# Attention heads of two key-value groups in turn, value products of both interleaved, and norm squares moved ahead of the forms

## The chip, the cores and the metric

One core of a Trainium2 chip runs the whole program. The metric is device microseconds of one execution, the median over runs; lower is better. The engines are TensorE (PE; its weight loads are PEld), VectorE (DVE), ScalarE (ACT), GpSimd (POOL) and SyncE (SP), which issues the transfers. Each works through its own list of instructions in order and waits on semaphores that others count up.

## The reference

A two-layer encoder trunk over two sequences, 528 and 272 tokens long (512 and 256 plus 16 learned meta tokens), width 1024, all in fp32. Cut to what matters here:

```python
for layer in range(2):
    h = h + 0.5 * swiglu(rms_norm(h, norm_ffn1[layer]), gate, up, down)   # width 2816
    hn = rms_norm(h, norm_mix[layer])
    h = h + (even_mixer(hn, ...) if layer % 2 == 0 else fourier_mixer(hn, ...))
    h = h + 0.5 * swiglu(rms_norm(h, norm_ffn2[layer]), gate, up, down)
return rms_norm(h, norm_final)[:, N_META:]
...
# even_mixer: attention of 8 heads of 64, heads 0-3 share key-value group 0, heads 4-7 group 1,
# window of 128 to either side, ALiBi bias, and a sink logit of each head in the softmax:
s = einsum(q, k) * scale + bias
m = maximum(max(s), sink); p = exp(s - m); denom = sum(p) + exp(sink - m)
o = einsum(p, v) / denom
```

The attention's result and a pooling mixer are concatenated and go through one output projection.

## The kernel before

Activations lie transposed: channels on the 128 partitions, 800 tokens along the free axis (h has 8 tiles of channels). Large products are three fp32r matmuls of high and low parts (w_hi, w_lo, and the same of the activations). ScalarE makes the high parts, VectorE the low ones.

The four feed-forward networks (f = 0 to 3) compute gate and up products by a Strassen scheme of seven products per tile of 128 columns (22 tiles), from sums of token and channel blocks ("forms" T1, T2, T3, N4, each with a high and a low part). The first two tiles of each network (the lead) are plain products: `plain_unit(j, u)`, 24 matmuls each and four per tile. They cover the making of the forms and of the norm: ScalarE squares the 8 channel tiles (`squares`), VectorE adds them (`add_square`, seven additions), TensorE sums over partitions (`statistics`), VectorE makes the variance, GpSimd raises it to -0.5 (`power`), VectorE spreads it to a diagonal (`diagonal`, into acth), TensorE broadcasts it (`broadcast`), VectorE copies it to rstd (`spread`). For f = 1 and 2 (EARLY) the squares are made in the stage before. For f = 0 and 3 they are made in the lead (`late_squares`), between the other steps of `lead`, in an order written out by hand on ScalarE and VectorE. There TensorE runs the four units of tile 0, the statistics, unit 0 of tile 1, the broadcast, and units 1 to 3; unit 2 waits for rstd. `weights_to(k)` on either engine makes the high or low parts (and sums) of the weights up to a few units ahead of k.

The attention works through 8 tiles of up to 128 queries (ATT_TILES; 256, 384, 384, 272 and 144 keys for the first sequence, 256, 272 and 144 for the second; the tiles of 144 keys have 16 queries), 8 heads each: 64 units u, in quads of four. For each unit: TensorE makes the scores (L1654; q_sb and k_sb hold group 0 in partitions 0 to 63 and group 1 in 64 to 127) into one of three banks; VectorE adds the bias and takes the maximum (L1357), per quad the negated maximum (L1366); ScalarE the exponential with its sum (L865) and that of the sink (L870); VectorE the denominator (L1380), its reciprocal and the scaling (L1387, `norm_quad`); TensorE transposes blocks of 128 keys (L1668) into one of two banks; ScalarE copies them to prob_t (L883, L886); and per quad TensorE multiplies by v (L1689, `times_v`), four heads side by side in up to 512 columns, output in partitions 64 times the group. TensorE's list runs the scores 8 units ahead of the transposes:

```python
for u in range(NU + AHEAD):
    if u < NU:
        scores(u)
    v = u - AHEAD
    if v >= 0:
        transposes(v)
        if v % 4 == 1 and v > 4:
            times_v(v // 4 - 1)
```

ScalarE's list is the exponentials of quad q, then the copies of quad q - 1. VectorE's is three scores of quad q, `norm_quad(q - 1)`, the fourth score, the negated maximum. Score buffer u % 8 is free when transposes(u - 8) are done. Banks 5 to 7 take the value products; from there ScalarE and VectorE write mx_hi and mx_lo (L893, L1394). Behind the attention come the pooling products (L1718 to L1722) and the output projection.

Of the kernel before, what the change touches and what calls it, by code (L numbers as in the profile page):

```python
# [8 lines left out]
P = 128  # L9
# [205 lines left out]
def build(nc, x, gains, sinks, ident_in, alibi_in, edges_in, pool_w_in, tables, gate_up, down5, down6,  # L215
# [18 lines left out]
    def as32(ap):  # L234
# [41 lines left out]
    projected = 6 * T + 4 * POOL_W  # L276
    (_, xn_hi, xn_lo, q_sb, k_sb, v_sb, u_pad, _, mx_hi, mx_lo) = scope([
        ("w_lo_m", [P, WL], f32),
        ("xn_hi", [P, KD, T], f32r), ("xn_lo", [P, KD, T], f32r),
        ("q_sb", [P, 4, T], f32), ("k_sb", [P, T], f32), ("v_sb", [P, T], f32),  # L280
        ("u_pad", [P, 4, POOL_W], f32), ("fill_m", [P, 2 * XF - 2 * KD * T - projected], f32),
        ("mx_hi", [P, KD, T], f32r), ("mx_lo", [P, KD, T], f32r)])
    (_, v_tok, prob_t, score, row_max, neg_max, sink_d, row_sum, sink_e, rden) = scope([
        ("w_lo_a", [P, WL], f32),
        ("v_tok", [P, len(ATT_TILES), P], f32), ("prob_t", [P, 2, 3, 4, P], f32),
        ("score", [P, SCORES, KEYS], f32), ("row_max", [P, 2, 4], f32), ("neg_max", [P, 2, 4], f32),
# [190 lines left out]
    norm_done = sem("norm_done")  # L477
    quad_out = sem("quad_out")
    mix_hi_done = sem("mix_hi_done")
# [29 lines left out]

    UNITS = [(i, hd) for i in range(len(ATT_TILES)) for hd in range(N_HEADS)]  # L510

# [110 lines left out]
    def _(act):  # L622
# [119 lines left out]
        def lead(f):  # L742

            n0, n1, J = GU[f][0], GU[f][1], f * FF_TILES
            early = f in EARLY
            weights_to(n0)
            late_squares(f, 0, 3)
            t1_gain(f)
            weights_to(n0 + 1)
            late_squares(f, 3, 5)  # L750
            form_high(f, "T1")
            late_squares(f, 5, 7)
            weights_to(n0 + 2)
            form_high(f, "T2")
            late_squares(f, 7, KD)
            weights_to(n0 + 3)
# [116 lines left out]
        def prob_copy(u):  # L873
            i = u // 8
            rows = ATT_TILES[i][3]
            k0, k1 = keys_of(i)
            q, c = divmod(u, 4)
            act.wait_ge(prob_t_ps, u + 1)
            if c == 0 and q >= 2:
                act.wait_ge(quad_out, q - 1)  # L880
            full, kr = divmod(k1 - k0, P)
            if kr:
                A.activation(prob_t[0:kr, q % 2, full, c, 0:rows],  # L883
                             banks[0:kr, 3 + u % 2, full * P:full * P + rows], ACT.Copy)\
                    .then_inc(prob_t_done, 1)
            A.activation(prob_t[:, q % 2, 0:full, c, 0:rows],  # L886
                         banks[:, 3 + u % 2, 0:full * P].rearrange("p (j r) -> p j r", r=P)[:, :, 0:rows],
                         ACT.Copy).then_inc(prob_t_done, 1)

        def out_hi(i):  # L890
            s0, L, t, rows = ATT_TILES[i]
            act.wait_ge(quad_out, 2 * i + 2)
            A.activation(mx_hi[:, 0:4, s0 + t:s0 + t + rows],  # L893
                         banks[:, 5 + i % 3, :].rearrange("p (k r) -> p k r", k=4)[:, :, 0:rows],
                         ACT.Copy).then_inc(mix_hi_done, 1)
# [58 lines left out]
    def _(dve):  # L954
# [186 lines left out]
        def ffn(f, norm_before, norm_after):  # L1141
# [40 lines left out]
            def lead():  # L1182

                n0, n1, J = GU[f][0], GU[f][1], f * FF_TILES
                early = f in EARLY
                weights_to(n0)
                late_squares(f, 0, 3)
                t1_sum(f)
                weights_to(n0 + 1)
                late_squares(f, 3, 5)  # L1190
                t2_sum(f)
                if early:
                    variance(norm_before)
                late_squares(f, 5, 7)
                weights_to(n0 + 2)
                if early:
                    diagonal(norm_before)
                form_low(f, "T1")
                late_squares(f, 7, KD)
                weights_to(n0 + 3)  # L1200
                if early:
# [141 lines left out]
        def score_quad(q):  # L1343
# [5 lines left out]
            for c in range(4):  # L1349
                u = 4 * q + c  # L1350
                hd = u % 8
# [5 lines left out]
                V.tensor_tensor_reduce(out=score[0:rows, u % SCORES, 0:k1 - k0],  # L1357
                                       in0=banks[0:rows, u % 3, 0:k1 - k0],
                                       in1=alibi[0:rows, hd, off:off + k1 - k0], scale=1.0,
                                       scalar=sink[0:rows, hd:hd + 1], op0=ALU.add, op1=ALU.max,  # L1360
                                       accum_out=row_max[0:rows, q % 2, c:c + 1])\
# [28 lines left out]
        def tile_lo(i):  # L1390
# [3 lines left out]
            V.tensor_tensor(mx_lo[:, 0:4, s0 + t:s0 + t + rows],  # L1394
                            banks[:, 5 + i % 3, :].rearrange("p (k r) -> p k r", k=4)[:, :, 0:rows],
                            as32(mx_hi[:, 0:4, s0 + t:s0 + t + rows]),
# [86 lines left out]
    def _(pe):  # L1483
# [163 lines left out]
        def scores(u):  # L1647
# [11 lines left out]
        def transposes(u):  # L1659
# [6 lines left out]
            for j in range((k1 - k0 + P - 1) // P):  # L1666
                kr = min(P, k1 - k0 - j * P)
                ins = M.transpose(banks[0:kr, 3 + u % 2, j * P:j * P + rows],  # L1668
                                  score[0:rows, u % SCORES, j * P:j * P + kr],
                                  ident[0:rows, 0:rows])  # L1670
            ins.then_inc(prob_t_ps, 1)

        def times_v(q):

            i = q // 2
            s0, L, t, rows = ATT_TILES[i]
            k0, k1 = keys_of(i)
            side = 64 * (q % 2)
            pe.wait_ge(prob_t_done, TCOUNT[4 * q + 4])
            if q == 0:  # L1680
# [251 lines left out]
```

## Time and profile before

| | |
|---|---|
| median of 3 runs | 2569.61 us (2568.35 to 2571.15) |
| profiled execution | 2569.58 us, span 2567.8 us |
| mean granted TensorE clock | 0.98 |
| busy: PE, DVE, ACT | 98%, 63%, 39% of the span |
| chain that ended last | PE 74%, issue 20%, DVE 3%, ACT 2% |
| attention stage | 641.6 to 757.6 us |
| opening of network 0, of network 3 | first 62 us; about 2010 to 2065 us |

The span is the time from the first to the last instruction of one execution on the chip; the profiled execution's own time is 1.8 us longer. Time on the chain that ended last is what a change can shorten; work of an engine beside it costs nothing. The granted clock is 1.00 at 2.4 GHz and 0.50 at 1.2 GHz.

### The profile page before, as it was taken

What the parts mean: (1) busy time and instruction counts of PE and PEld (TensorE: products, weight loads), DVE (VectorE), ACT (ScalarE), POOL (GpSimd) and SP (SyncE); (2) the same over time, 40 slices, a digit from 0 to 9 for tenths busy, and PEclk for the clock granted to TensorE, in tenths of its full rate; (3) what the DMA queues carried; (4) which work ended last, traced back from release to release, by engine and by line L of the source; (5) the groups of instructions that cost most, each with busy time, mean ns of one, the idle gap of its engine ahead of it and who ended that gap; (6) DMA issues with size and microseconds to landing.
All of it is one profiled execution on the core that took longest, in us unless ns stands there. A gap on an engine that the chain in (4) does not pass through costs nothing.

```text
span 2567.8 us, 35298 instructions
## 1 busy us (share of the span) xinstructions
PE 2504.8 (98%) x13740; PEld 2425.3 (94%) x13740; DVE 1621.7 (63%) x2858; ACT 1001.7 (39%) x1913; POOL 80.9 (3%) x85
## 2 busy tenths in 40 slices
PE   7999999999999999999999999999999899999997
PEld 7999999999449999999999999999999799999996
DVE  7665766753544757575677656665755775666574
ACT  5433433431553434242444433342443443434341
POOL 0000000014000000000000000000002100000000
PEclk9999999999889999999999999999999899999998
DMA  3211121221001121112121112121121211211121
GB/s 119 74 66 58 66 83 52 81 96 53 14 1 50 50 75 60 64 66 72 61 71 62 60 64 74 66 66 66 69 68 47 84 58 66 74 66 66 66 70 64
DMA packets 28532, 166.26 MB, mean 65 GB/s; under 512 B 3408, under 2 KB 3664, under 8 KB 16080
## 3 DMA queue, kind: packets, MB, share of 16 engines
q1 hardware_dynamic: 28368, 164.02, 18.3%
q8 instruction: 110, 1.80, 0.3%
q14 instruction: 54, 0.44, 0.1%
HBM read 160.73 MB, written 3.28 MB: 64 GB/s over the span
## 4 chain that ended last, share of the span: by engine, by line
PE 74%; issue 20%; DVE 3%; ACT 2%; DMA 0%; POOL 0%; POOLq 0%; DVEq 0%; SPq 0%; ACTq 0%
PE banks L1497 28%; PE banks L1576 12%; PE banks L1575 12%; PE banks L1574 12%; PE banks L1593 3%; PE banks L1490 2%; PE banks L1654 2%; PE banks L1689 1%; PE banks L1668 1%; ACT xf_hi L687 1%; DVE xf_lo L1027 0%; DVE sum_sq_x L1013 0%; PE banks L1526 0%; PE banks L1536 0%; DVE w_lo L981 0%
## 5 line engine op out<-in xcount | busy, mean ns | idle before, releaser
L1575 PE MATMUL banks<-xf_lo,w_hi 128*128 128x400 f32 (+2 forms) x2240 | 766.9, 342 | 0.0
L1576 PE MATMUL banks<-xf_hi,w_lo 128*128 128x400 f32 (+2 forms) x2240 | 765.0, 342 | 0.0
L1574 PE MATMUL banks<-xf_hi,w_hi 128*128 128x400 f32 (+2 forms) x2240 | 764.2, 341 | 0.0
L643 ACT ACTIVATE w_hi<-raw 128x512 fp32r<-128x512 f32 (+3 forms) x572 | 314.6, 560 | 365.5 <-PE banks L1497 365.5
L1576 PEld LDWEIGHTS banks<-xf_hi,w_lo 128*128 128x128 f32 x2240 | 422.4, 189 | 0.0
L1575 PEld LDWEIGHTS banks<-xf_lo,w_hi 128*128 128x128 f32 x2240 | 420.5, 188 | 0.0
L1574 PEld LDWEIGHTS banks<-xf_hi,w_hi 128*128 128x128 f32 x2240 | 420.1, 188 | 0.0
L1497 PE MATMUL banks<-act_hi,w_lo 128*128 128x400 f32 (+2 forms) x1408 | 366.4, 341 | 0.0
L1497 PE MATMUL banks<-act_lo,w_hi 128*128 128x400 f32 (+2 forms) x1408 | 366.2, 341 | 0.0
L1497 PE MATMUL banks<-act_hi,w_hi 128*128 128x400 f32 (+2 forms) x1408 | 365.7, 341 | 0.0
L981 DVE TENSOR_TENSOR w_lo<-raw,w_hi 128x512 fp32r<-128x512 f32 (+3 forms) x572 | 343.9, 615 | 19.5 <-ACT w_hi L643 19.4
L643 ACT ACTIVATE w_hi<-w_sum 128x512 fp32r<-128x512 f32 x336 | 209.9, 629 | 304.3 <-DVE w_sum L973 117.8
L1497 PEld LDWEIGHTS banks<-act_hi,w_hi 128*128 128x128 f32 x1408 | 258.5, 188 | 0.0
L1497 PEld LDWEIGHTS banks<-act_lo,w_hi 128*128 128x128 f32 x1408 | 258.1, 188 | 0.0
L1497 PEld LDWEIGHTS banks<-act_hi,w_lo 128*128 128x128 f32 x1408 | 258.0, 188 | 0.0
L981 DVE TENSOR_TENSOR w_lo<-w_sum,w_hi 128x512 fp32r<-128x512 f32 x336 | 229.5, 686 | 2.1 <-ACT w_hi L643 2.1
L1168 DVE TENSOR_TENSOR act_lo<-act,act_hi 128x800 fp32r<-128x800 f32 (+2 forms) x88 | 86.1, 979 | 175.9 <-ACT act_hi L740 175.9
L1137 DVE SCALAR_TENSOR_TENSOR h<-banks,h 128x392 f32<-128x392 f32 (+3 forms) x224 | 72.5, 383 | 133.2 <-PE banks L1497 133.2
L1131 DVE SCALAR_TENSOR_TENSOR h<-banks,h 128x800 f32<-128x800 f32 x64 | 63.4, 990 | 134.1 <-PE banks L1497 134.1
L790 ACT ACTIVATE g<-banks 128x400 f32<-128x400 f32 (+2 forms) x80 | 40.1, 501 | 208.7 <-PE banks L1576 208.7
L965 DVE TENSOR_TENSOR w_sum<-raw 128x512 f32<-128x512 f32 x80 | 55.0, 687 | 81.3 <-PE banks L1497 50.5
L740 ACT ACTIVATE act_hi<-act 128x800 fp32r<-128x800 f32 (+2 forms) x88 | 75.3, 856 | 35.4 <-DVE act L1162 35.4
(179 smaller groups left out, 2711.7 us busy)
## 6 DMA issues: line engine op xcount, KB each, us to landing
raw<-gate_up_dram SPq DMA_DIRECT2D x86, 1024.0 KB, 4.8
raw<-down_dram SPq DMA_DIRECT2D x32, 768.0 KB, 4.2
raw<-down_dram SPq DMA_DIRECT2D x32, 640.0 KB, 3.8
raw<-w_in_dram SPq DMA_DIRECT2D x5, 1024.0 KB, 4.8
raw<-w_fourier_dram SPq DMA_DIRECT2D x8, 576.0 KB, 3.8
raw<-w_out_dram SPq DMA_DIRECT2D x4, 1024.0 KB, 4.8
h<-x_dram SPq DMA_DIRECT2D x8, 400.0 KB, 7.2
y_dram<-h SPq DMA_DIRECT2D x8, 400.0 KB, 2.5
```

What stands on the lines that cost most here:

```text
L643: A.activation(w_hi[:, n % NS, 0:u.cols], source, ACT.Copy).then_inc(w_hi_done, 1)
L740: A.activation(act_hi[:, t, 0:W], act32[:, t, 0:W], ACT.Copy).then_inc(act_hi_done, 1)
L965: ins = V.tensor_tensor(out, quarter(u, "A21"), quarter(u, "A22"), ALU.add)
L981: V.tensor_tensor(w_lo[:, n % NS, 0:u.cols], source, as32(w_hi[:, n % NS, 0:u.cols]), ALU.subtract).then_inc(w_ready, 1)
L1131: return V.scalar_tensor_tensor(two(h[:, m, :]), slot(2 + m % 2), 0.5, two(h[:, m, :]), ALU.mult, ALU.add)
L1137: last = V.scalar_tensor_tensor(h[:, m, t:t + n], banks[:, 4 + 2 * (m % 2) + half, c:c + n], 0.5, h[:, m, t:t + n], ALU.mult, ALU.add)
L1168: V.tensor_tensor(act_lo[:, t, 0:W], act32[:, t, 0:W], as32(act_hi[:, t, 0:W]), ALU.subtract).then_inc(act_ready, 1)
L1497: ins = M.matmul(banks[:, bank + half, 0:cols], a, b[:, half * cols:(half + 1) * cols], start=first and j == 0, stop=last and j == 2)
L1574: M.matmul(out, a_hi, b_hi, start=fresh and k == 0, stop=False, skip_group_check=True)
L1575: M.matmul(out, a_hi, b_lo, start=False, stop=False, skip_group_check=True)
L1576: ins = M.matmul(out, a_lo, b_hi, start=False, stop=k == KP - 1, skip_group_check=True)
L1593: ins = M.matmul(banks[:, bank + half, 0:C], a_lo if p == 2 else a_hi, b, start=kind[2] == "1" and k == 0 and p == 0, stop=kind[2] == "2" ...
```

## The change

Attention: the eight heads of a tile are taken in the order 0, 4, 1, 5, 2, 6, 3, 7, so that neighbours belong to different key-value groups. Scores are issued two units at a time, with one wait for both, into four banks instead of three; there are 16 score buffers instead of 8, and prob_t holds two whole tiles (v_tok moves to another place in SBUF). The value products are made once per tile instead of once per quad, the two groups in turn for each block of keys, into two banks instead of three. Openings of networks 0 and 3: the squares and their additions are made ahead of T1's gain, T2 and the high and low parts; the networks 1 and 2 keep their order. N4 of networks 0 and 3 moves behind the diagonal.

```diff
-SCORES = 8
+SCORES = 16
+HEAD_ORDER = (0, 4, 1, 5, 2, 6, 3, 7)
...
-    UNITS = [(i, hd) for i in range(len(ATT_TILES)) for hd in range(N_HEADS)]
+    UNITS = [(i, hd) for i in range(len(ATT_TILES)) for hd in HEAD_ORDER]
...
 # ScalarE, lead(f); the order for early stays
+            else:
+                late_squares(f, 0, 4)
+                weights_to(n0 + 1)
+                late_squares(f, 4, KD)
+                t1_gain(f)
+                weights_to(n0 + 2)
+                form_high(f, "T1")
+                weights_to(n0 + 3)
+                form_high(f, "T2")
...
 # ScalarE, prob_copy(u)
-            if c == 0 and q >= 2:
-                act.wait_ge(quad_out, q - 1)
+            if u % N_HEADS == 0 and i >= 2:
+                act.wait_ge(tile_out, i - 1)
...
 # VectorE, lead()
                 else:
-                    less_t2(f, "N4")
-
-                if not early:
+                    late_squares(f, 0, 3)
+                    t1_sum(f)
+                    late_squares(f, 3, 6)
+                    weights_to(n0 + 1)
+                    late_squares(f, 6, KD)
+                    weights_to(n0 + 2)
+                    t2_sum(f)
+                    weights_to(n0 + 3)
+                    form_low(f, "T1")
                     variance(norm_before)
+
                 weights_to(n1)
                 if early:
                     plain_gate(0, J)
                 else:
                     diagonal(norm_before)
+                    less_t2(f, "N4")
...
 # TensorE, scores(u)
-            if u >= 3:
-                pe.wait_ge(score_done, u - 2)
-            M.matmul(banks[0:rows, u % 3, 0:k1 - k0],
+            M.matmul(banks[0:rows, u % 4, 0:k1 - k0],
...
-        def times_v(q):
+        def times_v(i):
...
-            pe.wait_ge(prob_t_done, TCOUNT[4 * q + 4])
+            pe.wait_ge(prob_t_done, TCOUNT[N_HEADS * (i + 1)])
...
-            if q % 2 == 0 and i >= 3:
-                pe.wait_ge(mix_ready, i - 2)
+            if i >= 2:
+                pe.wait_ge(mix_ready, i - 1)
...
             for j in range(n):
                 kr = min(P, k1 - k0 - j * P)
-                out = banks[side:side + 64, 5 + i % 3, :].rearrange("p (k r) -> p k r", k=4)
-                ins = M.matmul(out[:, :, 0:rows], v_tok[0:kr, tile0 + j, side:side + 64],
-                               prob_t[0:kr, q % 2, j, :, 0:rows], start=j == 0, stop=j == n - 1)
-            ins.then_inc(quad_out, 1)
+                for side in range(2):
+                    rows_of = slice(64 * side, 64 * side + 64)
+                    out = banks[rows_of, 6 + i % 2, :].rearrange("p (k r) -> p k r", k=4)
+                    ins = M.matmul(out[:, :, 0:rows], v_tok[0:kr, tile0 + j, rows_of],
+                                   prob_t[0:kr, i % 2, side, j, :, 0:rows], start=j == 0, stop=j == n - 1)
+            ins.then_inc(tile_out, 1)
...
-        for u in range(NU + AHEAD):
+        for u in range(0, NU + AHEAD, 2):
             if u < NU:
+                if u >= 4:
+                    pe.wait_ge(score_done, u - 2)
                 scores(u)
+                scores(u + 1)
             v = u - AHEAD
             if v >= 0:
                 transposes(v)
-                if v % 4 == 1 and v > 4:
-                    times_v(v // 4 - 1)
-        times_v(NU // 4 - 1)
+                transposes(v + 1)
+                if v % N_HEADS == 2 and v > N_HEADS:
+                    times_v(v // N_HEADS - 1)
+        times_v(len(ATT_TILES) - 1)
```

## Rows read from the trace of the kernel before

**Rows 1.** The page, part 4: shares of the chain that ended last

```profile
PE 74%; issue 20%; DVE 3%; ACT 2%; DMA 0%; POOL 0%; POOLq 0%; DVEq 0%; SPq 0%; ACTq 0%
```

**Rows 2.** Stretches of the attention: length, busy (count) by engine, PEclk, DMA share, GB/s

```profile
641.60:757.60 116.00, 113.46 (x370) 46.51 (x370) 60.01 (x263) 62.75 (x251) 0.00 (x0) 0.81 0.02 9
...
641.60:665.50 23.90, 23.48 (x47) 10.14 (x48) 11.25 (x46) 10.69 (x37) 0.00 (x0) 0.50 0.09 38
...
716.70:737.20 20.50, 20.36 (x50) 8.65 (x48) 9.37 (x41) 9.73 (x42) 0.00 (x0) 0.50 0.00 1
```

**Rows 3.** Waits of VectorE, 641 to 757 us: total us, times, longest

```profile
DVE score L1357 <- PE banks L1668: 47.1, 20, 4.4
```

**Rows 4.** Timeline, first scores: start, us, engine, line, op, out<-in, count [idle<-releaser]

```profile
643.07 1.06 PE L1654 MATMUL banks<-k_sb,q_sb 64*128 64x256 f32 x2
...
644.71 1.22 PE L1654 MATMUL banks<-k_sb,q_sb 64*128 64x256 f32 x4
```

**Rows 5.** Groups by line, whole span: out<-in, shapes, count | busy us, mean ns | idle

```profile
L1654 PE MATMUL banks<-k_sb,q_sb 64*128 64x272 f32 (+3 forms) x128 | 53.4, 530 | 0.0
...
L1689 PE MATMUL banks<-prob_t,v_tok 128*64 128x512 f32 (+3 forms) x80 | 37.0, 589 | 0.4 <-ACT prob_t L886 0.4
...
L1668 PE MATMUL banks<-ident,score 128*128 128x128 f32 (+3 forms) x160 | 31.2, 297 | 2.2 <-ACT prob_t L886 1.0 <-DVE score L1387 0.4 <-ACT prob_t L883 0.3
```

**Rows 6.** Weight loads of L1689: duration ns least/median/most, first and last start

```profile
L1689 PEld LDWEIGHTS banks<-prob_t,v_tok x80: 127/137/231, 661.3 to 757.4; 128*64 128x64 f32 x64, 16*64 16x64 f32 x16
```

**Rows 7.** Timeline of TensorE, one stretch at half and one at full clock

```profile
661.28 3.68 PE L1689 MATMUL banks<-prob_t,v_tok 128*64 128x512 f32 x4
...
672.04 0.91 PE L1654 MATMUL banks<-k_sb,q_sb 64*128 64x384 f32 x2
672.88 0.55 PE L1668 MATMUL banks<-ident,score 128*128 128x128 f32 x3
...
677.31 2.79 PE L1689 MATMUL banks<-prob_t,v_tok 128*64 128x512 f32 x6
```

**Rows 8.** Timeline of VectorE and ScalarE, one quad of 384 keys

```profile
676.50 0.17 DVE L1366 TENSOR_SCALAR neg_max<-row_max 128x4 f32<-128x4 f32 x1
...
679.11 0.19 ACT L870 ACTIVATE sink_e<-sink_d 128x4 f32<-128x4 f32 x1
...
682.11 0.16 DVE L1380 TENSOR_TENSOR rden<-row_sum,sink_e 128x4 f32<-128x4 f32 x1
...
684.49 0.17 DVE L1366 TENSOR_SCALAR neg_max<-row_max 128x4 f32<-128x4 f32 x1
```

**Rows 9.** Timeline, opening of the first network

```profile
22.50 1.85 DVE L1037 TENSOR_TENSOR xf<-h 128x544 f32<-128x544 f32 x2
...
29.87 2.75 DVE L1049 SCALAR_TENSOR_TENSOR xf<-h,gain,xf 128x136 f32<-128x136 f32 x8
...
35.14 1.78 DVE L1077 TENSOR_TENSOR xf_lo<-xf,xf_hi 128x1568 fp32r<-128x1568 f32 x1
...
37.88 2.83 PE L1526 MATMUL banks<-ones,sum_sq_x 128*100 128x1 f32 x16 [6.82 <-DVE sum_sq_x L1013]
...
41.06 1.95 POOL L531 TENSOR_TENSOR rstd_tok<-var,minus_half 100x8 f32<-100x8 f32 x1 [40.08 <-DVE var L1106]
...
46.77 0.69 DVE L968 TENSOR_TENSOR w_sum<-w_sum,raw 128x512 f32<-128x512 f32 x1 [2.73 <-PE banks L1593]
```

**Rows 10.** The chain that ended last, first network: start, us, what

```profile
40.70 6.03 PE banks L1593 x24
...
48.05 12.80 PE banks L1593 x72
```

**Rows 11.** Timeline of TensorE, opening of the last network

```profile
2040.13 2.83 PE L1526 MATMUL banks<-ones,sum_sq_x 128*100 128x1 f32 x16 [9.28 <-DVE sum_sq_x L1013]
...
2049.38 1.46 PE L1536 MATMUL banks<-acth,ones 100*128 100x384 f32 x6
```

**Rows 12.** A stretch of the last network's opening, columns as in rows 2

```profile
2034.30:2047.90 13.60, 7.77 (x32) 7.77 (x33) 10.76 (x16) 3.94 (x6) 2.03 (x1) 0.50 0.18 64
```

More of the change, by code:

```diff
@@ L276, in build @@
     projected = 6 * T + 4 * POOL_W
-    (_, xn_hi, xn_lo, q_sb, k_sb, v_sb, u_pad, _, mx_hi, mx_lo) = scope([
+    rest = 2 * XF - 2 * KD * T - projected - len(ATT_TILES) * P
+    (_, xn_hi, xn_lo, q_sb, k_sb, v_sb, u_pad, v_tok, _, mx_hi, mx_lo) = scope([
         ("w_lo_m", [P, WL], f32),
@@ L280, in build @@
         ("q_sb", [P, 4, T], f32), ("k_sb", [P, T], f32), ("v_sb", [P, T], f32),
-        ("u_pad", [P, 4, POOL_W], f32), ("fill_m", [P, 2 * XF - 2 * KD * T - projected], f32),
+        ("u_pad", [P, 4, POOL_W], f32), ("v_tok", [P, len(ATT_TILES), P], f32), ("fill_m", [P, rest], f32),
         ("mx_hi", [P, KD, T], f32r), ("mx_lo", [P, KD, T], f32r)])
-    (_, v_tok, prob_t, score, row_max, neg_max, sink_d, row_sum, sink_e, rden) = scope([
+    (_, prob_t, score, row_max, neg_max, sink_d, row_sum, sink_e, rden) = scope([
         ("w_lo_a", [P, WL], f32),
-        ("v_tok", [P, len(ATT_TILES), P], f32), ("prob_t", [P, 2, 3, 4, P], f32),
+        ("prob_t", [P, 2, 2, 3, 4, P], f32),
         ("score", [P, SCORES, KEYS], f32), ("row_max", [P, 2, 4], f32), ("neg_max", [P, 2, 4], f32),
@@ L477, in build @@
     norm_done = sem("norm_done")
-    quad_out = sem("quad_out")
+    tile_out = sem("tile_out")
     mix_hi_done = sem("mix_hi_done")
@@ L873, in prob_copy @@
         def prob_copy(u):
-            i = u // 8
+            i, hd = UNITS[u]
+            side, c = divmod(hd, 4)
             rows = ATT_TILES[i][3]
             k0, k1 = keys_of(i)
-            q, c = divmod(u, 4)
             act.wait_ge(prob_t_ps, u + 1)
-            if c == 0 and q >= 2:
-                act.wait_ge(quad_out, q - 1)
+            if u % N_HEADS == 0 and i >= 2:
+                act.wait_ge(tile_out, i - 1)
             full, kr = divmod(k1 - k0, P)
             if kr:
-                A.activation(prob_t[0:kr, q % 2, full, c, 0:rows],
-                             banks[0:kr, 3 + u % 2, full * P:full * P + rows], ACT.Copy)\
+                A.activation(prob_t[0:kr, i % 2, side, full, c, 0:rows],
+                             banks[0:kr, 4 + u % 2, full * P:full * P + rows], ACT.Copy)\
                     .then_inc(prob_t_done, 1)
-            A.activation(prob_t[:, q % 2, 0:full, c, 0:rows],
-                         banks[:, 3 + u % 2, 0:full * P].rearrange("p (j r) -> p j r", r=P)[:, :, 0:rows],
+            A.activation(prob_t[:, i % 2, side, 0:full, c, 0:rows],
+                         banks[:, 4 + u % 2, 0:full * P].rearrange("p (j r) -> p j r", r=P)[:, :, 0:rows],
                          ACT.Copy).then_inc(prob_t_done, 1)
@@ L891, in out_hi @@
             s0, L, t, rows = ATT_TILES[i]
-            act.wait_ge(quad_out, 2 * i + 2)
+            act.wait_ge(tile_out, i + 1)
             A.activation(mx_hi[:, 0:4, s0 + t:s0 + t + rows],
-                         banks[:, 5 + i % 3, :].rearrange("p (k r) -> p k r", k=4)[:, :, 0:rows],
+                         banks[:, 6 + i % 2, :].rearrange("p (k r) -> p k r", k=4)[:, :, 0:rows],
                          ACT.Copy).then_inc(mix_hi_done, 1)
@@ L1186, in lead @@
                 weights_to(n0)
[L1187 to L1191, printed above, removed]
                 if early:
+                    t1_sum(f)
+                    weights_to(n0 + 1)
+                    t2_sum(f)
                     variance(norm_before)
-                late_squares(f, 5, 7)
-                weights_to(n0 + 2)
-                if early:
+                    weights_to(n0 + 2)
                     diagonal(norm_before)
[L1198 to L1201, printed above, removed]
+                    form_low(f, "T1")
+                    weights_to(n0 + 3)
                     less_t2(f, "T3")
@@ L1204, in lead @@
                 else:
-                    less_t2(f, "N4")
-                if not early:
+                    late_squares(f, 0, 3)
+                    t1_sum(f)
+                    late_squares(f, 3, 6)
+                    weights_to(n0 + 1)
+                    late_squares(f, 6, KD)
+                    weights_to(n0 + 2)
+                    t2_sum(f)
+                    weights_to(n0 + 3)
+                    form_low(f, "T1")
                     variance(norm_before)
@@ L1350, in score_quad @@
                 u = 4 * q + c
-                hd = u % 8
+                hd = UNITS[u][1]
                 if c == 3 and q:
@@ L1357, in score_quad @@
                 V.tensor_tensor_reduce(out=score[0:rows, u % SCORES, 0:k1 - k0],
-                                       in0=banks[0:rows, u % 3, 0:k1 - k0],
+                                       in0=banks[0:rows, u % 4, 0:k1 - k0],
                                        in1=alibi[0:rows, hd, off:off + k1 - k0], scale=1.0,
-                                       scalar=sink[0:rows, hd:hd + 1], op0=ALU.add, op1=ALU.max,
+                                       scalar=sink[0:rows, u % N_HEADS:u % N_HEADS + 1], op0=ALU.add, op1=ALU.max,
                                        accum_out=row_max[0:rows, q % 2, c:c + 1])\
@@ L1394, in tile_lo @@
             V.tensor_tensor(mx_lo[:, 0:4, s0 + t:s0 + t + rows],
-                            banks[:, 5 + i % 3, :].rearrange("p (k r) -> p k r", k=4)[:, :, 0:rows],
+                            banks[:, 6 + i % 2, :].rearrange("p (k r) -> p k r", k=4)[:, :, 0:rows],
                             as32(mx_hi[:, 0:4, s0 + t:s0 + t + rows]),
@@ L1667, in transposes @@
                 kr = min(P, k1 - k0 - j * P)
-                ins = M.transpose(banks[0:kr, 3 + u % 2, j * P:j * P + rows],
+                ins = M.transpose(banks[0:kr, 4 + u % 2, j * P:j * P + rows],
                                   score[0:rows, u % SCORES, j * P:j * P + kr],
@@ L1671, in transposes @@
             ins.then_inc(prob_t_ps, 1)
-        def times_v(q):
-            i = q // 2
+        def times_v(i):
             s0, L, t, rows = ATT_TILES[i]
             k0, k1 = keys_of(i)
-            side = 64 * (q % 2)
-            pe.wait_ge(prob_t_done, TCOUNT[4 * q + 4])
-            if q == 0:
+            pe.wait_ge(prob_t_done, TCOUNT[N_HEADS * (i + 1)])
+            if i == 0:
                 pe.wait_ge(v_tok_done, len(ATT_TILES))
-            if q % 2 == 0 and i >= 3:
-                pe.wait_ge(mix_ready, i - 2)
+            if i >= 2:
+                pe.wait_ge(mix_ready, i - 1)
             n = (k1 - k0 + P - 1) // P
@@ L1878 @@
     gains = np.concatenate(norms).reshape(-1, P).T
-    sinks = np.broadcast_to(a["attn_sink"][0][None, :], (P, N_HEADS))
+    sinks = np.broadcast_to(a["attn_sink"][0][list(HEAD_ORDER)][None, :], (P, N_HEADS))
     def pairs(blocks):
```

13 lines of the change are left out of this document (3 added, 10 removed).

## The prediction

> **What bounds the kernel now.** I read the page's chain first: [rows 1] give TensorE 74% of the span and "issue" 20%, so only time on TensorE counts, and that of VectorE and ScalarE where TensorE waits for them. Then the attention stage, which most of the diff touches [rows 2]: TensorE is busy 113.5 of 116.0 us, though its granted clock is only 0.81; VectorE works 60.0 us and ScalarE 62.8. VectorE waits there 47.1 us in 20 waits for transposes [rows 3]. The reader should see one engine that fills 116 us and two that need some 60 and wait for it. Last the openings of the first and last network, the other part of the diff: TensorE waits 6.8 and 9.3 us for the norm's sum of squares [rows 9, 11].
>
> **Score products in pairs (HEAD_ORDER, four score banks).** Heads 0 to 3 read partitions 0 to 63, heads 4 to 7 partitions 64 to 127. Before, every unit is followed by a transpose, and neighbours of different halves meet only among the first eight. There the trace shows what they do [rows 4]: two matmuls of one half take 1.06 us, but the four of heads 3 and 4 take 1.22 together (in series 1.91, since the next one starts 0.43 behind the last). Different halves run side by side, in fp32. After the change each pair is issued together: for 384 keys about the 0.84 us that one unit takes now (672.04 to 672.88 in [rows 7]), 1.6 at half clock. Half of the 53.4 us of [rows 5] falls away.
>
> The Trainium skill ("TensorEngine Tiling (Array Packing)", Key Properties) says that a change of tiling mode drains the array. Pairs halve the number of changes, and the 0.84 us contain one, so the sum stays the same by either.
>
> **Value products.** 64 matmuls of 512 columns, 0.45 us each at full clock (2.79 us for six) and 0.92 at half (3.68 for four) [rows 7], and 16 small ones. Now side 0 and side 1 alternate; they write partitions 0 to 63 and 64 to 127 of one bank, and both read all 128 rows. No row shows two column halves at once. Bounds: side by side, 32 x 0.45 = 14.5 us less at full clock; in series nothing less, and if each change of side also showed its weight load of 0.14 us [rows 6], 9 us more. I take side by side, as the row halves do in rows 4. The skill ("TensorE: Matmul & The Clock Gate", Part 3) gives 2.38 times for three column tiles; at that efficiency two halves would cost some 3 us more than I count. No run here shows it.
>
> **What TensorE then costs.** [rows 5]: 53.4 / 2 + 31.2 + 37.0 / 2 = 76 us at a clock of 0.81, so 62 at full clock, as much as VectorE's 60. The bound moves to the loop between VectorE and ScalarE. For a quad of 384 keys [rows 8]: negated maximum at 676.50, four exponentials and the sink's on ScalarE until 679.30, 2.80 us; then VectorE divides, scales four units and makes the fourth score: 682.11 to the next maximum at 684.49, 2.38 us. 5.2 us instead of 8.0.
>
> **The sum for the attention**, relative to before:
> - VectorE's 47.1 us of waits go.
> - Back comes the wait for the exponentials: 2.80 us in a quad against 2.3 of three scores and the small steps, 0.5 us in 15 quads: +7.5.
> - Back comes a new wait. A tile's value products stand in one block between transposes and the next scores. In the odd quad, counted from its maximum: ScalarE's copies come behind the exponentials, the first at +3.3 us; two transposes, 0.5 each, to +4.4; the block of twelve matmuls, 2.7, to +7.1; a pair of scores to +7.9; two transposes and a pair to +9.7, two scores of VectorE later the norm starts at +10.4 where the exponentials end at +8.0. So 2.4 us for each of four large tiles, about 1 for the two of 256 keys: +11.6.
> - The opening stays at half clock until the first value products, and there TensorE stays the bound (1.6 + 2 x 0.95 us for a pair of units): +5. The first maximum comes 1.4 us earlier, as heads 1 and 3 come with 0 and 2.
> - At the end the block of the seventh tile falls behind the last maximum: +2.
> Sum: -47.1 + 7.5 + 11.6 + 5 - 1.4 + 2 = -22.4 us if the clock is full behind the opening.
> - Clock: it stood at 0.50 (1.2 GHz) from 641.6 to 665.5 and for 20.5 us from 716.7, on a TensorE that was never idle [rows 2]; before it fell there, it did score products of 64 rows and narrow transposes. After, TensorE is idle some 3 us in most tiles. I assume 20.5 us at half again behind the opening. A tile of 384 keys takes there 19 us of TensorE work (4 x 1.6 + 8 x 0.95 + 5.5) instead of the 2 x 5.2 + 2.4 = 12.8 above, so 20.5 us lose 6.8.
> Attention: about -16 us. Bounds: -22.4 with the clock full; 0 with all of it at half, for then TensorE's 2 x 62 us fill the old 116.
>
> Edits at nothing: v_tok and the wider score and prob_t only move in SBUF. Two output banks instead of three make tile i wait for the subtraction of tile i-2, which VectorE issues ten units earlier. The sink vector is only reordered. The 16 score buffers are what ends the 47.1 us.
>
> **The first network's opening** [rows 9, 10]. TensorE ends its first tile at 37.88 - 6.82 = 31.06 and waits for the seventh addition. On VectorE the additions stand behind T1's sum, T2's sum (2.75 us) and T1's low part (1.78). Now: two additions to 22.5, T1's sum to 24.3, three additions of 1.0 to 27.3, one w_lo of 0.6 to 28.0, two additions to 30.1; ScalarE's squares keep up, as its gains (2.2 us) now follow them. The statistics start at 31.06 at full clock, half of 2.8 us, and the 24 matmuls behind them take 24 x 0.178 = 4.3 us (12.80 / 72) instead of 6.0: TensorE is at 36.7. What is late next is the diagonal: on VectorE w_lo to 30.7, T2's sum to 33.4, w_lo to 34.0, T1's low part to 35.8, the variance to 36.0, then GpSimd's power of 2.0 and the diagonal's 1.0: 39.1. TensorE waits 2.5 us and broadcasts at 39.3 instead of 46.7: -7.4 us. N4's 2.2 us and two weight steps now stand between diagonal and the copy of rstd, which is made at 43.6, before the third unit wants it at 44.6. T2's low part comes some 12 us behind the broadcast, wanted after 17 (96 matmuls of 0.178); VectorE had waited 2.73 us for TensorE there [rows 9], which covers N4. The weight loads wait on SP's queue for the w_lo of their last unit, which comes no later.
>
> **The last network's** [rows 11, 12]. Wait of 9.28 us up to 2040.13, broadcast at 2049.38, half clock from 2034.3 to 2047.9. The same order gives the additions by 2032.3 (a wait of 1.5 us), TensorE through its 24 matmuls at 2037.9, the diagonal at 2041.2 after another wait of 3.3: broadcast at 2041.3, -8.1 us. This wait may drop the clock again; the 7.8 us of work at half cost 3.9 before, I take half of it, +2.
> Openings: -7.4 - 8.1 + 2 = -13.5 us. Bounds: -15.5, and -8 if the clock falls in both new waits.
>
> **Forecast.** -16 - 13.5 = -29.5 us. The profiled execution took 2569.58 us (span 2567.8 and 1.8 around it), the median of the runs is 2569.61. So 2540 us; own range 2530 to 2552 (attention -24 to -8, openings -15.5 to -9).
>
> **Rivals.**
> - The clock stays full behind the opening (12%): denser scores speak for it, the new idle time against. -22.4 - 13.5: 2534.
> - The clock is at half for nearly all the attention (14%): rows 2 show it falling without any idle time. Attention 0: 2556. The skill ("TensorE: Matmul & The Clock Gate", HAM oscillation) says that idle gaps between bursts bring the clock back to half; by that rule this would be the likelier case.
> - Value products in series, loads hidden (10%): the block is 5.4 us, each large tile waits 2.7 us more, the others 1.9, part of it at half clock: +16, 2556.
> - Slower than before (4%): the two column halves exclude each other and each change of side shows its load. At half clock 64 x (0.92 + 0.23) = 74 us of blocks instead of 14.5, 2600; at full clock 64 x 0.59, 2563; between them 2578. It decides from 0.7 us per matmul on, for 64 x 0.7 - 14.5 is the 30 us gained elsewhere.
> - The openings bring next to nothing, because diagonal and clock take it back (4%): 2554.
> - What is left, within 0.2% (4%).
> The forecast has 52%. The range 2528 to 2560 holds all but the slower case and the last. A measurement of this kernel tells 0.2% (5 us) from no change. Faster 0.92, same 0.04, slower 0.04.
>
> **What would show it.** After: waits for sum_sq_x under 2 us in all, and a wait for the diagonal (acth) of 2 to 3.5 us in each opening; VectorE's waits for transposes nearly gone; TensorE idle before transposes that wait for prob_t; score matmuls starting in pairs; twelve value matmuls in 2.7 us; the stage about 100 us long. The forecast is wrong if twelve value matmuls take 5.4 us, if the granted clock of the stage is under 0.6, or if a late form stalls the first products of tile 2.

## The result: 2540 us, 1.2% faster, and the profile after

The changed kernel takes 2539.97 us (median of 4 runs, 2538.2 to 2541.21), the kernel before 2569.05 beside it (2568.35 to 2571.15, 4 runs). The ratio is 0.988 (95% interval 0.9866 to 0.9893): 29 us, where 29.5 were forecast. The spans of the profiled executions are 2567.8 and 2539.1 us, 28.7 apart.

The attention stage is the larger part. From the first score to the first pooling product it took 115.6 us before (642.05 to 757.62), now 99.0 (635.25 to 734.22). The stretch of the changed kernel that answers to the first of [rows 2], with three stretches inside it (length, busy and count for PE, PEld, DVE, ACT, POOL, then granted clock, DMA share, GB/s):

```profile
635.20:734.20 99.00, 74.19 (x369) 32.82 (x368) 59.53 (x263) 61.86 (x250) 0.00 (x0) 0.80 0.02 10
643.20:650.00 6.80, 4.95 (x18) 2.44 (x16) 4.60 (x20) 5.67 (x22) 0.00 (x0) 0.50 0.00 0
...
670.50:673.90 3.40, 3.40 (x9) 1.00 (x10) 1.33 (x6) 2.76 (x11) 0.00 (x0) 0.50 0.02 5
684.10:687.50 3.40, 3.40 (x10) 0.72 (x6) 0.20 (x2) 1.79 (x9) 0.00 (x0) 0.50 0.00 0
```

TensorE is busy 74.2 us instead of 113.5, and VectorE and ScalarE do the work they did before. No engine fills the stage now: VectorE, ScalarE and TensorE wait for each other in turn. The granted clock is 0.80, as before (0.81), but its half stretches are short pieces and not two long ones. The waits show who is late (total us, times, longest), first TensorE's, then VectorE's:

```profile
PE banks L1676 <- ACT prob_t L894: 18.0, 9, 2.6
...
PE banks L1546 <- DVE acth L1122: 5.2, 3, 3.0
...
PE banks L1662 <- DVE row_max L1367: 4.2, 8, 0.7
```

```profile
DVE score L1367 <- PE banks L1662: 26.7, 14, 4.0
...
DVE rden L1390 <- ACT sink_e L878: 6.2, 8, 1.2
```

VectorE's 47.1 us of waits for transposes [rows 3] are gone. In their place it waits 26.7 us for score products. Those are not slow themselves: they stand on TensorE behind the value block, which stands behind transposes that wait for ScalarE's copies. One such place on TensorE's timeline:

```profile
666.37 0.73 PE L1662 MATMUL banks<-k_sb,q_sb 64*128 64x272 f32 x4 [0.65 <-DVE row_max L1367]
669.67 0.89 PE L1676 MATMUL banks<-ident,score 128*128 128x128 f32 x6 [2.57 <-ACT prob_t L894]
670.49 4.46 PE L1697 MATMUL banks<-prob_t,v_tok 128*64 128x512 f32 x12
674.89 0.73 PE L1662 MATMUL banks<-k_sb,q_sb 64*128 64x272 f32 x4
```

The block of twelve takes 4.46 us and not 2.79, because the clock stands at 0.50 (1.2 GHz) from 670.5 to 673.9, right behind a wait of 2.57 us.

In the openings the statistics and the broadcast answer to [rows 9] and [rows 11]:

```profile
30.47 1.57 PE L1536 MATMUL banks<-ones,sum_sq_x 128*100 128x1 f32 x16 [0.56 <-DVE sum_sq_x L1021]
39.84 1.59 PE L1546 MATMUL banks<-acth,ones 100*128 100x392 f32 x6 [1.88 <-DVE acth L1122]
...
2011.20 2.22 PE L1536 MATMUL banks<-ones,sum_sq_x 128*100 128x1 f32 x16 [1.58 <-DVE sum_sq_x L1021]
2020.51 1.57 PE L1546 MATMUL banks<-acth,ones 100*128 100x384 f32 x6 [0.30 <-DVE acth L1122]
```

The first broadcast is 6.7 us earlier than before. In the last network the way from the end of the first tile's products to the broadcast shrinks from 18.5 us (2040.13 - 9.28 = 2030.85 to 2049.38) to 10.9 (2011.20 - 1.58 = 2009.62 to 2020.51), 7.6 us less. Together -6.7 - 7.6 - 16.6 = -30.9 us. Between the stage and the last network 2.2 us of that are given back, 2.1 of them right behind the stage. The output projection starts 11.01 us behind the first pooling product (734.22 to 745.23) instead of 10.45 (757.62 to 768.07), at half clock until 738.7 where the kernel before is at half until 761.1. The projection's first twelve products then take 3.85 us instead of 2.28, at half clock from 745.6 to 749.0 where the kernel before is at full.

### The profile page after: what moved, and what is told of

It is laid out like the page before. It is cut to its first block, busy times and chain, and to the rows that moved or that the text cites. A ratio compares the mean times of both kernels' runs of the same rounds, so it can differ in the third digit from the quotient of the medians.

```text
span 2539.1 us, 35283 instructions
## 1 busy us (share of the span) xinstructions
PE 2467.7 (97%) x13740; PEld 2412.8 (95%) x13740; DVE 1621.8 (64%) x2858; ACT 1000.8 (39%) x1913; POOL 81.8 (3%) x85
## 3 DMA queue, kind: packets, MB, share of 16 engines
q1 hardware_dynamic: 28368, 164.02, 18.5%
## 4 chain that ended last, share of the span: by engine, by line
PE 72%; issue 21%; DVE 4%; ACT 2%; DMA 0%; POOL 0%; POOLq 0%; SPq 0%; DVEq 0%; ACTq 0%
PE banks L1507 29%; PE banks L1586 12%; PE banks L1585 12%; PE banks L1584 12%; PE banks L1603 3%; PE banks L1500 2%; PE banks L1697 1%; ACT score L873 1%; DVE sum_sq_x L1021 1%; PE banks L1676 1%; PE banks L1662 0%; ACT xf_hi L690 0%; DVE w_lo L989 0%; DVE xf_lo L1035 0%; PE banks L1546 0%
## 5 line engine op out<-in xcount | busy, mean ns | idle before, releaser
L743 ACT ACTIVATE act_hi<-act 128x800 fp32r<-128x800 f32 (+2 forms) x88 | 75.3, 856 | 35.1 <-DVE act L1170 35.1
```

Source lines behind the costliest of these rows:

```text
L743: A.activation(act_hi[:, t, 0:W], act32[:, t, 0:W], ACT.Copy).then_inc(act_hi_done, 1)
```

## The experiments

All were built on the changed kernel unless said otherwise, and each was set against the kernel before on the same chip. One thing bears on all stage lengths below: where the half clock falls differs between executions. The changed kernel's stage took 99.0 us at a granted clock of 0.80, and 96.1 at 0.83 when the same kernel was profiled again; so a stage that is 3 us longer or shorter proves nothing by itself.

**One half of the change at a time.** The first kernel has the attention's edits and the old opening, the second the openings' edits on the kernel before.

> The attention part alone, with the lead of the kernel before. Reading of the two traces: the attention stage went from 115.6 to 99.0 us (-16.6) and the stretch behind it gave 2.2 us back, so about -14.4 us: 2554.6. Rival (the two parts overlap, or one of them carries nearly all): under -10 or over -20 us.

> The openings of the first and last network alone, with the attention of the kernel before. From the traces: -6.7 us in the first, -7.6 in the last, so about -14.3 us: 2554.7, and together with the attention alone -28.7. Rival (a later form or weight stalls TensorE and takes part of it back): the time saved up to the broadcast is 14 us but the whole gains less than 10.

Attention alone: 2552.05 us against 2569.59, -17.5 (ratio 0.9932, 0.9917 to 0.9947), its stage 95.5 us long. Openings alone: 2558.97, -10.6 (ratio 0.996, 0.9944 to 0.9976). The two add up to -28.1, against -29.1 for the whole: within the intervals the halves are independent. Against the prediction's -16 and -13.5 the attention gave 1.5 more and the openings 2.9 less. Against the 14.3 us by which the two broadcasts come earlier, the openings' 10.6 are also less; the interval (6 to 14 us) is too wide to say whether something takes the rest back.

**Pairs from one half of the rows.** The pairs stay, but both heads of a pair read the same 64 partitions:

```diff
-HEAD_ORDER = (0, 4, 1, 5, 2, 6, 3, 7)
+HEAD_ORDER = (0, 1, 2, 3, 4, 5, 6, 7)
```

> The changed kernel with the heads in their natural order: the pairs of scores then lie in one half of the array, all else stays (16 buffers, one wait for a pair, value products as changed). Theory (score products of different halves run side by side and this carries part of the gain): a pair takes 0.64 us more at full clock, 32 pairs 16 us of TensorE's work, half of it on the path: the stage 6 to 10 us longer, 2546 to 2550. Rival (the 16 buffers alone freed VectorE, and TensorE has 25 us of idle time in the stage anyway): no change, 2540.

2547.36 us (ratio 0.9914, 0.9899 to 0.9929), 7.4 above the changed kernel. A pair of 384 keys, first in the changed kernel and then in this one, both at full clock:

```profile
639.08 0.92 PE L1662 MATMUL banks<-k_sb,q_sb 64*128 64x384 f32 x4 [0.51 <-DVE row_max L1367]
```

```profile
668.60 1.55 PE L1662 MATMUL banks<-k_sb,q_sb 64*128 64x384 f32 x4
```

So the pairing across the two halves is worth some 5 to 7 us: 7.4 by the whole times, 4.9 by the stage (103.9 us). Part of that may be the clock, for this stage's is 0.75. Its saving of TensorE's time is larger (93.5 us busy in this run's stage, 74.2 in the changed kernel's), but most of that falls into waits.

**Value products one side after the other.** The loop over `side` is put outside the loop over key blocks:

```diff
-            for j in range(n):
-                kr = min(P, k1 - k0 - j * P)
-                for side in range(2):
+            for side in range(2):
+                for j in range(n):
+                    kr = min(P, k1 - k0 - j * P)
```

> The changed kernel with the value products of group 0 first, then those of group 1, so that neighbours write the same partitions, except where the groups meet. Theory (column halves run side by side, and the 4.5 us of a block of twelve after the change is half clock): a block at full clock takes 5.4 us instead of 2.7, and the stage 14 us more or somewhat less: 2550 to 2556. Rival (they run in series already and 4.5 us is what twelve cost): 2540.

2545.41 us (ratio 0.9912, 0.9896 to 0.9929), +5.4, where 10 to 16 were expected. Two blocks of this kernel:

```profile
671.32 5.37 PE L1697 MATMUL banks<-prob_t,v_tok 128*64 128x512 f32 x12
...
729.44 7.43 PE L1697 MATMUL banks<-prob_t,v_tok 128*64 128x512 f32 x12
```

The block at 671.32 costs only 0.9 us more than the interleaved one at 670.49, the one at 729.44 2.9 more than its match (4.57). So the written order is not the order in which they run. By its records, in the block at 671.32 side 1's first matmul starts together with side 0's third. The eight matmuls of a tile of 256 keys even take the same 1.94 us at full clock (at 721.52) as they take interleaved in the next experiment. The two blocks of 272 keys did run one by one: the one at 696.47 took 5.79 us at a granted clock of 1.00, where the interleaved one takes 2.94 at full clock (684.98 in the next experiment), and the one at 729.44 took 7.43 with 3.4 us of it at half. That is the price of a true series, 2.85 us for a block of twelve. As most blocks overlapped anyway, the interleaving is worth only 5.4 us here.

**The value block in the transposes' wait.** If the block costs what it does because it comes behind the wait for `prob_t`, it can go ahead of those two transposes: it reads older copies, so it can fill the wait.

```diff
+                if v % N_HEADS == 2 and v > N_HEADS:
+                    times_v(v // N_HEADS - 1)
                 transposes(v)
                 transposes(v + 1)
-                if v % N_HEADS == 2 and v > N_HEADS:
-                    times_v(v // N_HEADS - 1)
```

> The changed kernel with one step of TensorE's list moved: a tile's value products ahead of the two transposes that wait for ScalarE's copies, instead of behind them. After the change that wait is 2.4 to 2.6 us in each tile, the block of value products comes behind it, at half clock, 4.5 us, and the next scores behind the block. Theory (the block behind the wait delays VectorE's third score, and the clock falls because of the wait): the block fills the wait, runs at full clock in 2.7 us, and the stage loses 2 to 3 us for each of six tiles: -12 to -18 us against the changed kernel, 2522 to 2528. Rival A (the clock does not depend on that wait): the order gives about -8 us, the blocks stay at 4.5 us: 2532. Rival B (the loop of VectorE and ScalarE already sets the pace): 2540.

2523.43 us (2520.6 to 2526.95, ratio 0.9807, 0.9785 to 0.9828): 16.5 us less than the changed kernel, which had run on another chip. With both on one chip, further down, the difference is 19.0 us. Its stage takes 79.8 us (636.85 to 716.68), 19.2 less. The timeline at the block of the place shown above, and the windows of the whole stage and of its half-clock stretches:

```profile
665.84 0.73 PE L1662 MATMUL banks<-k_sb,q_sb 64*128 64x272 f32 x4
666.50 2.79 PE L1697 MATMUL banks<-prob_t,v_tok 128*64 128x512 f32 x12
669.23 0.87 PE L1676 MATMUL banks<-ident,score 128*128 128x128 f32 x6
```

```profile
645.40:652.20 6.80, 5.51 (x18) 2.73 (x19) 4.18 (x17) 5.31 (x20) 0.00 (x0) 0.50 0.00 0
693.20:700.00 6.80, 5.67 (x27) 3.07 (x25) 4.86 (x21) 5.79 (x24) 0.00 (x0) 0.50 0.00 0
636.85:716.68 79.83, 62.68 (x370) 29.94 (x369) 59.70 (x263) 60.53 (x250) 0.00 (x0) 0.91 0.03 12
```

No wait stands in front of the block, the clock stays full over it, and the block falls from 4.46 to 2.79 us. That figure also answers what no row of before could: the two column halves run side by side at full rate, twelve matmuls in the time that six took alone [rows 7]. VectorE's maxima show who sets the pace now, first in the changed kernel, then in this one:

```profile
666.35 0.17 DVE L1376 TENSOR_SCALAR neg_max<-row_max 128x4 f32<-128x4 f32 x1
671.53 0.17 DVE L1376 TENSOR_SCALAR neg_max<-row_max 128x4 f32<-128x4 f32 x1
679.57 0.17 DVE L1376 TENSOR_SCALAR neg_max<-row_max 128x4 f32<-128x4 f32 x1
```

```profile
665.53 0.17 DVE L1376 TENSOR_SCALAR neg_max<-row_max 128x4 f32<-128x4 f32 x1
670.70 0.17 DVE L1376 TENSOR_SCALAR neg_max<-row_max 128x4 f32<-128x4 f32 x1
675.27 0.17 DVE L1376 TENSOR_SCALAR neg_max<-row_max 128x4 f32<-128x4 f32 x1
```

The first step takes 5.2 us in both, as worked out from [rows 8]. The next one, whose scores stand behind the block in the changed kernel, takes 8.04 us there and 4.57 here, the pace of the loop between VectorE and ScalarE.

How much of the gain is order and how much is clock? Other profiles answer this. When the changed kernel was profiled again, the block at this place stood behind the same wait of 2.57 us and ran at full clock (671.52, 2.79 us); the step took 6.38 us. So of the 3.5 us, 1.8 are the order and 1.7 the half clock over the block. And the moved block was profiled three more times, in the versions below: stages of 79.5 us at a granted clock of 0.91, 82.2 at 0.85 and 83.5 at 0.81. The last has the changed kernel's clock and is still 15.5 us shorter than its 99.0. Most of the gain is the order; the clock accounts for some 4 us, and moving the block does not guarantee it.

**Eight score buffers.** `SCORES = 8` as before, everything else as changed.

> The changed kernel with 8 score buffers as before, pairs and value products as changed. VectorE's score of unit u then waits for the transposes of unit u - 8, and for the third of a quad these wait for ScalarE's copies behind its exponentials. Theory (the buffers are what takes VectorE's 47 us of waits away): some 1.8 us back in each of 16 quads, VectorE's wait for transposes above 25 us again, 2558 to 2566. Rival (TensorE's shorter work alone frees VectorE): under 2545.

2549.18 us (ratio 0.9908, 0.9886 to 0.9929), +9.2 on another chip than the changed kernel, whose interval (up to 0.9893) it just overlaps. The direction holds, the size was overrated. The wait for transposes is back, 36.3 of the 47.1 us:

```profile
DVE score L1367 <- PE banks L1676: 36.3, 20, 4.6
```

But it only takes the place of the 26.7 us for the score products: what VectorE waits in all grows by some 7 us, which is the length that the stage grows by (106.2 against 99.0). Its granted clock is 0.73 instead of 0.80, so part of the growth may be the clock.

**The variance earlier.** In the first and last network the diagonal was the next late thing. This kernel takes the variance 2.9 us earlier in VectorE's order:

```diff
                     t2_sum(f)
+                    variance(norm_before)
                     weights_to(n0 + 3)
                     form_low(f, "T1")
-                    variance(norm_before)
```

> The changed kernel with the variance of the first and last network ahead of one weight's low part and of T1's low part on VectorE (2.35 us). Theory (what is late next is the diagonal): TensorE's waits for it in the two openings, 1.9 to 2.9 us and 0.3 to 1.9 us in the runs so far, go to nearly nothing: 2 to 4 us less, 2536 to 2538. Rival (TensorE would wait for the next step, the copy of rstd or a form): 2540.

2543.23 us (ratio 0.9883, 0.9863 to 0.9904): nothing gained, and a miss. The variance was there at 33.05, and the diagonal still began at 38.25. GpSimd's power, the step between them, shows why; in the changed kernel, and in this one:

```profile
36.22 2.54 POOL L534 TENSOR_TENSOR rstd_tok<-var,minus_half 100x8 f32<-100x8 f32 x1 [35.24 <-DVE var L1114]
```

```profile
33.37 4.85 POOL L534 TENSOR_TENSOR rstd_tok<-var,minus_half 100x8 f32<-100x8 f32 x1 [32.38 <-DVE var L1114]
```

The same operation on the same 100x8 elements lasts 4.85 us where VectorE goes on with four operations behind the variance, and ends 1.5 us behind the last of them, as it does behind the last of two in the changed kernel. Together with the value block's move it brings nothing either:

> Both moves of the two kernels above. If they add up: 12 to 18 and 2 to 4 us less than the changed kernel, 2519 to 2526.

2522.27 us (ratio 0.9798, 0.9773 to 0.9823), 1.2 from the version without it, inside both intervals; the moved block alone explains it.

**The diagonal at once.** To see whether VectorE's work stretches the power, VectorE is made to stand idle for it: the diagonal follows the variance, on the version with the moved value block. That version and the changed kernel ran again beside it.

```diff
                     t2_sum(f)
+                    variance(norm_before)
+                    diagonal(norm_before)
                     weights_to(n0 + 3)
                     form_low(f, "T1")
-                    variance(norm_before)
...
                 else:
-                    diagonal(norm_before)
                     less_t2(f, "N4")
```

> The changed kernel with the value block in the transposes' wait, and in the first and last network VectorE takes the variance and then the diagonal at once, before the low halves of the next weights and of the next tokens. Theory (GpSimd's power is held while VectorE runs operations with two operands in SBUF: it lasted 4.85 us beside them in the run with the variance early, against 1.95 in the kernel before): VectorE now stands idle for it, so the power lasts about 2.0 us, starts near 33.4 and the diagonal starts near 36.2 instead of 38.8; the broadcast starts near 37.3 instead of 39.87, TensorE gives back up to 1 us waiting for the low halves that come 3 us later. Over both openings -2 to -5 us: 2518 to 2522 us. Rival (the power's time varies by itself, 2.5 us and more in this place): diagonal at 37 or later, and the low halves' lateness takes the rest: 2523 us or above.

> The version with the value block ahead of the transposes again, on the same chip as its variants. Theory: 2523 us, the power 2.54 us and the diagonal at 38.8.

> The changed kernel again, on the same chip. Both theories: 2540 us, ratio 0.988 to the kernel before; the half-clock stretches behind each wait of 2.4 us or more for the copies of transposed weights appear again.

On one chip: the diagonal at once 2518.58 us (ratio 0.9801, 0.9787 to 0.9814), the moved block alone 2521.88 (0.9814, 0.9801 to 0.9828), the changed kernel 2540.86 (0.9885, 0.9871 to 0.9898), before 2571.47. The moved block is thus worth 19.0 us; its power took 2.55 us and its diagonal began at 37.84. The changed kernel's half-clock stretches appear again, but not behind each long wait as expected: four of the five waits of 2.27 to 2.57 us for `prob_t` are followed by one, that of 2.57 us before the block at 671.52 is not. The power and the diagonal of the first opening, with the diagonal at once:

```profile
33.26 1.64 POOL L534 TENSOR_TENSOR rstd_tok<-var,minus_half 100x8 f32<-100x8 f32 x1 [32.29 <-DVE var L1114]
```

```profile
34.94 0.99 DVE L1122 TENSOR_TENSOR acth<-ident,rstd_tok 100x800 f32<-100x800 f32 x1 [1.82 <-POOL rstd_tok L534]
35.85 0.68 DVE L989 TENSOR_TENSOR w_lo<-raw,w_hi 128x512 fp32r<-128x512 f32 x1
```

1.64 us beside an idle VectorE, 4.85 beside a busy one. The power of the last network goes the same way (4.90 and 1.65 us), and in the kernel before a power of the same size next to an idle VectorE also took 1.64 (at 558.92). The diagonal starts at 34.94, and the first broadcast at 35.98 where it is at 38.89 in the version without it. Then 1.89 us go to a new wait of the products for the copied broadcast. In the last network the way from statistics to broadcast falls only from 9.3 to 8.9 us, with TensorE waiting for nothing at the broadcast. So the power's length follows VectorE's work beside it; that it varies by itself, the rival, is out. The whole time is within the forecast of 2518 to 2522, but its 3.3 us against the version beside it lie in overlapping intervals.

## Why the prediction came out right

The total was 0.03 us off, which is luck: the clock and the rest of the attention's sum were both mis-sized and cancelled, and in part so did the openings, which saved 0.8 us more than forecast up to their broadcasts, and the 2.2 us given back behind the stage, which the sum did not have.

- **Score pairs across the halves.** Right: 0.92 us for a pair of 384 keys (0.85 between starts), and 1.55 with both heads in one half.
- **Value products side by side.** Right at full clock: 2.79 us for twelve against 2.7 in the sum. In series, the rival, is out. (The "some 3 us more" that the prediction gives for a loss of efficiency is 3.8 by its own figures, 14.5 x 3 / 2.38 - 14.5; the 2.79 us show no such loss.) The Trainium skill ("TensorEngine Tiling (Array Packing)", Key Properties) was taken to leave the sum as it was, and it did.
- **VectorE's 47.1 us of waits.** They went, and the runs with eight buffers and with the moved block say what they were worth: most of them moved into the next wait, 26.7 us for score products.
- **The late value block, +11.6.** The mechanism was right: the wait of transposes for ScalarE's copies, the block behind it, then the scores. From first to last maximum the changed kernel takes 75.3 us (637.85 to 713.11) and the version with the moved block 63.1 (639.44 to 702.49), 12.2 apart. But those 12.2 hold the half clock over the block too, which the sum had apart. On one chip, with the changed kernel's clock fuller (0.83), it is 73.6 against 62.8 us, 10.8 apart.
- **The opening at half clock, +5.** Wrong. The first pairs ran at full clock (two pairs of 256 keys in 1.14 us at 635.25, where one took 1.22 in [rows 4]), and the first half stretch begins at 643.2 behind idle time. It is not so in every execution: with the diagonal at once the clock is at half from 633.0 to 639.8.
- **The clock, 20.5 us at half behind the opening, +6.8.** Wrong in its place and amount. About 40 us of the stage are at half, in pieces of 3.4 to 6.8 us and one of 10.2 that runs on into the pooling. Those from 656.8, 670.5, 684.1 and 694.4 lie over value blocks, behind waits for `prob_t` of 2.4, 2.6, 2.6 and 1.5 us; a block of twelve loses 1.7 us by one (4.46 against 2.79), the block of eight at 657.7 1.2 (3.16 against 1.94). So the half clock, which I had expected where TensorE is never idle, came where it waits. But a wait alone does not decide: the clock stayed full behind 2.57 us in the second profile of the changed kernel (before 671.52) and behind 1.90 us with the block moved (before 663.56), and [rows 2] have it at half with next to no wait. The pieces from 714.9 and 728.5, and the waits around them, are the 6.9 us by which the changed kernel is longer than the moved block's from the last maximum on (21.1 against 14.2 us). (The tile's work in this term is 4 x 1.6 + 8 x 0.95 + 5.5 = 19.5 us and not 19, which makes it 7.0 instead of 6.8.)
- **Set against the sum:** opening, block, tail and clock were put at 5 + 11.6 + 2 + 6.8 = 25.4 us and measured 19.2 (99.0 - 79.8) by the moved block, which takes the late block away and, in that execution, most of the half clock with it. What is left was put at 116 - 47.1 + 7.5 - 1.4 = 75 us and measured 79.8, as TensorE still waits there 12.4 us for `prob_t` and twice runs at half. The errors of 6.2 and 4.8 us cancel.
- **Openings, -7.4 and -8.1, +2 for the clock.** Measured -6.7 and -7.6. The step that is off in the first is the power of 2.0 us, which took 2.54 (1.64 where VectorE stood idle); at half clock (32.2 to 35.6) TensorE also reached the broadcast later, so that its wait was 1.88 us and not 2.5. In the last, the wait for the diagonal was 0.30 us and not 3.3, for the half clock (2011.9 to 2018.7) filled it: the clock's loss and the wait are one time, not two terms. (The prediction bounds the openings by -8, but its range takes -9.)
- **Rivals.** The Trainium skill's rule on idle gaps ("TensorE: Matmul & The Clock Gate", HAM oscillation) named waits as what brings the half clock, and the trace agrees in part: every half stretch of the changed kernel's stage begins in a wait of 1.5 us or more or within 1.6 us of one, but not every such wait brings one. It was priced as the whole stage at half, which did not come; the stage's clock is 0.80.

What stays open is why the clock falls where it does. Behind the stage TensorE waits 2.10 us in both kernels before the output projection; behind this wait the clock is full in the kernel before and at half in the changed one. No run took one stretch alone away.

## What to carry to other kernels

Put work whose inputs are long ready in front of an instruction that has to wait, not behind it. One block of products moved ahead of the transposes brought 19 us here, two thirds of what the whole change brought, since it fills the wait and no longer delays what VectorE wants next; some 4 of the 19 are a fuller clock. When a wait of 47 us disappears, ask which one takes its place before counting it as gained. And before an operation is moved earlier, look at what runs on its neighbour engine there: the variance 2.9 us earlier gave a power 2.3 us longer.

## What the hardware showed that I had not expected

- GpSimd's power of 100x8 elements took 1.64 us beside an idle VectorE, 1.95 to 2.63 beside two of its operations and 4.85 beside four. The Trainium skill ("SBUF — State Buffer", "SBUF: two separate sides") has a rule for it: GpSimd and VectorE share a pair of ports that one instruction locks, and VectorE takes part in this when it has two inputs in SBUF. The trace agrees in direction; each of those operations has two inputs in SBUF. That VectorE's operations run back to back and GpSimd gets in only at the end is what the durations of 2.54 and 4.85 us suggest: both ended 1.5 us behind VectorE's last operation. It is not the whole rule: in the kernel before, beside the same two operations (40.82 to 42.12), the power took 1.95 us and ended 0.9 behind them. No run here explains that or separates kinds of VectorE operations.
- Value matmuls of the two column halves overlapped even where the program has one half's matmuls all ahead of the other's. A block of 256 keys ran as fast as interleaved (1.94 us for eight), blocks of 384 keys overlapped in part (5.37 us with 3.4 us at half clock, where the interleaved one took 4.46). The two blocks of 272 keys did not overlap and took 5.79 us at full clock and 7.43 with 3.4 us at half, against 2.94 interleaved. Their last block of keys has only 16 rows; so has that of the tiles of 144 keys, where eight small matmuls took 1.09 us instead of 0.59. Whether the 16 rows are the reason was not tried by itself.
